# Six raw weight slots in the context pass, and a third of its merge's low parts made by VectorE

## The reference, cut to what matters

```
p = h @ w_in                                   # one projection; its last 4 x 1024 columns are the merge gates
gates = sigmoid(merge_logits.reshape(b, n, 4, 1024))
total = 0.0
for i in range(4):                             # attention, convolution, retention, Fourier
    total = total + gates[:, :, i] * ((ys[i] * silu(zs[i])) @ w_os[i])
y = total @ w_out
```

## Time and profile before

| what | value |
|---|---|
| median of three runs | 2635.76 us |
| lowest and highest | 2635.73 and 2635.92 us |
| span of the profiled execution | 2630.7 us |
| time around the span, median less span | 5.1 us |
| PE busy | 95% of the span |
| POOL busy | 46%, 1114.0 us of it the 818 low parts |
| first gate to last gate of the first pass's merge | from 222.8 to 366.4 us |

### The profile page before, as it was taken

How to read it: one execution, slowest core, us unless ns; L and a number is a source line. 1 busy time by engine, 2 the same in 40 slices (tenths; PEclk the granted TensorE clock), 3 DMA queues, 4 the chain that set the end, 5 groups by cost and what they waited for, 6 DMA issues and landing times.

```text
span 2630.7 us, 39625 instructions
## 1 busy us (share of the span) xinstructions
PE 2498.0 (95%) x12993; PEld 2092.3 (80%) x12993; DVE 1144.0 (43%) x1698; ACT 1114.4 (42%) x2321; POOL 1218.1 (46%) x992
## 2 busy tenths in 40 slices
PE   7888989999999999999999989999999999999997
PEld 1887878799888767787888778898888788888886
DVE  2453565396254433333343365592535423333332
ACT  2645554396221554434433433694214433343332
POOL 1567873222222378855555442122213455555553
PEclk9999999999999999999999989999999999999999
DMA  6345653100121155544433431001211333344333
GB/s 239 93 131 176 197 164 104 40 1 18 48 64 31 57 148 158 158 123 140 137 108 105 140 116 48 13 1 41 62 38 28 108 108 112 111 141 139 109 112 120
DMA packets 391576, 262.37 MB, mean 100 GB/s; under 512 B 16006, under 2 KB 363286, under 8 KB 389914
## 3 DMA queue, kind: packets, MB, share of 16 engines
q1 hardware_dynamic: 377248, 227.07, 29.2%
q10 hardware_dynamic: 14204, 33.67, 3.6%
HBM read 251.23 MB, written 9.45 MB: 99 GB/s over the span
## 4 chain that ended last, share of the span: by engine, by line
PE 79%; issue 7%; POOL 6%; DVE 4%; ACT 2%; DMA 0%; DVEq 0%; POOLq 0%; ACTq 0%; SPq 0%
PE ps L680 76%; POOL w_lo L581 6%; PE ps L839 2%; DVE softmax_stats L1921 1%; DVE r_prev L2028 1%; DVE x_post L2253 0%; DVE a_probT_lo L1662 0%; DMA w_ada<-in_w_ada 0%; PE ps L779 0%; DVE a_out_sum L1662 0%; DVE norm_tmp L1807 0%; PE ps L825 0%; PE ps L712 0%; ACT a_prob L1349 0%; DVE x_post L1766 0%
## 5 line engine op out<-in xcount | busy, mean ns | idle before, releaser
L581 POOL TENSOR_TENSOR w_lo<-w_raw,w_hi 128x512 fp32r<-128x512 f32 x818 | 1114.0, 1373 | 1076.2 <-ACT w_hi L1174 1068.7
L680 PE MATMUL ps<-hT_hi,w_hi 128*128 128x512 f32 (+1 forms) x2528 | 946.1, 374 | 46.9 <-POOL w_lo L581 31.3
L1174 ACT ACTIVATE w_hi<-w_raw 128x512 fp32r<-128x512 f32 x818 | 507.8, 629 | 1010.9 <-PE ps L680 859.1
L680 PE MATMUL ps<-hT_lo,w_hi 128*128 128x512 f32 (+1 forms) x2528 | 932.7, 369 | 0.0
L680 PE MATMUL ps<-hT_hi,w_lo 128*128 128x512 f32 (+1 forms) x2528 | 932.6, 369 | 0.0
L680 PEld LDWEIGHTS ps<-hT_hi,w_hi 128*128 128x128 f32 x2528 | 482.2, 191 | 142.7 <-POOL w_lo L581 31.0
L680 PEld LDWEIGHTS ps<-hT_hi,w_lo 128*128 128x128 f32 x2528 | 482.3, 191 | 79.0
L680 PEld LDWEIGHTS ps<-hT_lo,w_hi 128*128 128x128 f32 x2528 | 482.5, 191 | 75.5
L1662 DVE TENSOR_TENSOR merge_tmp<-merge_tmp,ps 128x512 f32<-128x512 f32 (+1 forms) x160 | 101.5, 634 | 674.5 <-PE ps L680 412.5
L1662 DVE TENSOR_TENSOR merge_tmp<-merge_tmp 128x512 f32<-128x512 f32 (+1 forms) x120 | 168.8, 1406 | 4.1
L680 PE MATMUL ps<-yT_hi,w_hi 128*128 128x512 f32 (+1 forms) x400 | 148.1, 370 | 7.0 <-DVE merge_tmp L1662 3.4
(11 more groups left out here) (265 smaller groups left out, 2799.1 us busy)
## 6 DMA issues: line engine op xcount, KB each, us to landing
w_raw<-in_w_in SPq DMA_DIRECT2D x512, 256.0 KB, 2.9
w_raw<-in_w_o_rest SPq DMA_DIRECT2D x120, 256.0 KB, 2.7
w_raw<-in_w_out SPq DMA_DIRECT2D x80, 256.0 KB, 2.6
w_ada<-in_w_ada SPq DMA_DIRECT2D x8, 1536.0 KB, 9.4
w_raw<-in_w_ada SPq DMA_DIRECT2D x48, 256.0 KB, 2.8
w_raw<-in_w_o_attn SPq DMA_DIRECT2D x40, 256.0 KB, 2.8
w_raw<-in_dft_x SPq DMA_DIRECT2D x16, 256.0 KB, 2.7
gate_row<-gate_rows ACTq DMA_DIRECT2D x5, 512.0 KB, 3.9
```

Source lines behind the costliest of these rows:

```text
L581: eng.tensor_tensor(w_lo[:, r, :], raw[:, r, :], w_hi[:, r, :].bitcast(F32), ALU.subtract).then_inc(sem["w_split"], tally.up("w_split"))
L680: return eng.matmul(dst, lhsT, rhs, start=start, stop=stop)
L1174: return eng.activation(dst, src, func, **kw)
```

## The change

It has two parts. **Six raw slots:** in the first pass the raw ring has HEAD_RING = 6 slots. The two new ones lie in the unused right halves of tiles that the context pass fills only to 256 columns, so each is two pieces of 256 columns, and a unit in such a slot is loaded by two DMAs of half the size; ACT and the low part read it as two pieces in one instruction. SP waits for the unit six before. The first pass's loads and low parts are written out instead of looped. Two token tiles and a gate row are placed elsewhere to make room. **Low parts on VectorE:** in the first pass's merge the low part of each step's third unit, the w_o unit, is made by VectorE (`head_low` in the vector block, 32 of them), and counted on a semaphore of its own, `w_split_dve`. VectorE makes that of step n+1 right after it has added step n's product, ahead of the step's share of `early_norm`, and the first one before the merge's first step. GpSimd leaves these units out. PE and SP wait for the one or the other count.

```diff
+HEAD_RING = 6
...
+        raw_more = [at("w_raw_more0", [P, 2, 512], W + 8704)[:, :, 256:512], at("w_raw_more1", [P, 2, 2048], W + 7680)[:, :, 256:512]]
...
+        total_units, head_units = units, passes[0].units
+        def raw_slot(u):
+            return u % HEAD_RING if u < head_units else u % RING
+        def raw_unit(u):
+            r = raw_slot(u)
+            return raw[:, r, :] if r < RING else raw_more[r - RING]
...
+        def low_by_dve(u):
+            return 0 <= u - first_merge < 12 * KT and (u - first_merge) % 3 == 2
...
@@ sync
+            def free_from(u):
+                if u >= head_units + RING:
+                    eng.wait_ge(sem["w_split"], tally.take("w_split"))
+                    return
+                before = u - (RING if u >= head_units else HEAD_RING)
+                if before >= 0 and low_by_dve(before):
+                    eng.wait_ge(sem["w_split_dve"], dve_lows(before + 1))
+                elif before >= 0:
+                    eng.wait_ge(sem["w_split"], RING + before + 1 - dve_lows(before + 1))
...
-                eng.wait_ge(sem["w_split"], tally.take("w_split"))
+                free_from(u)
...
+                for half in range(2):
+                    if shape == k4:
+                        part, place = src[:, 2 * half:2 * half + 2, :], dst[:, half, :].rearrange("p (k n) -> p k n", n=P)
+                    else:
+                        part, place = src[:, half, :] if shape else src[:, half * 256:(half + 1) * 256], dst[:, half, :]
+                    eng.dma_start(place, part).then_inc(landed[r], tally.up(f"w_landed{r}", 16))
@@ gpsimd
+                while unit[0] < min(last, head_units):
+                    if low_by_dve(unit[0]):
+                        tally.skip("w_high", 1)
+                    else:
+                        head_low(unit[0])
+                    unit[0] += 1
@@ tensor
-                        r = slot()
+                        r = slot(p.opens)
@@ scalar
-                    eng.wait_ge(landed[r], tally.take(f"w_landed{r}", 16))
+                    eng.wait_ge(landed[raw_slot(u)], tally.take(f"w_landed{raw_slot(u)}", 16 if raw_slot(u) < RING else 32))
                     eng.wait_ge(sem["w_used"], tally.take("w_used"))
-                    act(w_hi[:, r, :], raw[:, r, :]).then_inc(sem["w_high"], tally.up("w_high"))
+                    act(split_like(w_hi[:, r, :], u), raw_unit(u)).then_inc(sem["w_high"], tally.up("w_high"))
@@ vector
+            def head_low(u):
+                r = u % RING
+                eng.wait_ge(sem["w_high"], u + 1)
+                tt(split_like(w_lo[:, r, :], u), raw_unit(u), split_like(w_hi[:, r, :], u).bitcast(F32),
+                   ALU.subtract).then_inc(sem["w_split_dve"], tally.up("w_split_dve"))
+
             def merge(p, b):
                 tmp = tmp_blk[b]
                 eng.wait_ge(sem["y_split"], tally.now("y_split"))
+                if p.opens:
+                    head_low(first_merge + 2)
...
                         if more:
                             tally.skip("w_used__done", 2)
+                        if p.opens and 4 * i + j + 1 < 4 * KT:
+                            head_low(first_merge + 3 * (4 * i + j + 1) + 2)
                         if latent:
                             early_norm(i, j)
```

More of the change, by code:

```diff
@@ L220, in trunk @@
         m_gpost = at("mod_gpost", [P, D], W + 6144)
-        m_gate = at("mod_gate", [P, D], W + 7168)
+        m_gate = at("mod_gate", [P, D], W + 12288)
         n_row = at("ada_row", [P, UNIT], Z + 3584)
@@ L334, in trunk @@
         sem = {n: ctx.enter_context(nc.semaphore(n)) for n in names}
-        landed = [ctx.enter_context(nc.semaphore(f"w_landed{r}")) for r in range(RING)]
+        landed = [ctx.enter_context(nc.semaphore(f"w_landed{r}")) for r in range(HEAD_RING)]
         x_in = [ctx.enter_context(nc.semaphore(f"x_in{t}")) for t in range(SEQ // P)]
@@ L380, in trunk, with split_like, dve_lows @@
             units += p.units
-        total_units = units
+        total_units, head_units = units, passes[0].units
[4 more added lines that the diff above has]
+            return raw[:, r, :] if r < RING else raw_more[r - RING]
+        def split_like(t, u):
+            return t if raw_slot(u) < RING else t.rearrange("p (a n) -> p a n", a=2)
+        first_merge = 2 * len(passes[0].tiles) + passes[0].dft
+        def low_by_dve(u):
+            return 0 <= u - first_merge < 12 * KT and (u - first_merge) % 3 == 2
+        def dve_lows(count):
+            return sum(low_by_dve(u) for u in range(count))
         def feeds_next(p, b):
@@ L482, in _ @@
             unit = [0]
+            k4 = {"k": 4, "n": P}
+            def free_from(u):
[7 more added lines that the diff above has]
+                    eng.wait_ge(sem["w_split"], RING + before + 1 - dve_lows(before + 1))
+                if not low_by_dve(u):
+                    tally.take("w_split")
             def load(source, shape=None):
                 src = source() if callable(source) else source
-                r = unit[0] % RING
+                u = unit[0]
+                r, dst = raw_slot(u), raw_unit(u)
                 unit[0] += 1
-                dst = raw[:, r, :]
-                if shape:
+                if r < RING and shape:
                     dst = dst.rearrange(f"p ({' '.join(shape)}) -> p {' '.join(shape)}", **shape)
-                eng.wait_ge(sem["w_split"], tally.take("w_split"))
+                free_from(u)
                 if tally.i is not None:
                     eng.sem_inc(sem["w_slot"], 1)
-                eng.dma_start(dst, src).then_inc(landed[r], tally.up(f"w_landed{r}", 16))
+                if r < RING:
+                    eng.dma_start(dst, src).then_inc(landed[r], tally.up(f"w_landed{r}", 16))
+                    return
+                for half in range(2):
[4 more added lines that the diff above has]
+                    eng.dma_start(place, part).then_inc(landed[r], tally.up(f"w_landed{r}", 16))
             def rounds(times, body, units):
+                if unit[0] < head_units:
+                    for i in range(times):
+                        body(i)
+                    return
                 assert units % RING == 0
@@ L582, in low @@
                                   ALU.subtract).then_inc(sem["w_split"], tally.up("w_split"))
+            def head_low(u):
+                r = u % RING
+                eng.wait_ge(sem["w_high"], tally.take("w_high"))
+                eng.tensor_tensor(split_like(w_lo[:, r, :], u), raw_unit(u), split_like(w_hi[:, r, :], u).bitcast(F32),
+                                  ALU.subtract).then_inc(sem["w_split"], tally.up("w_split"))
             unit = [0]
             def low_parts(last):
+                while unit[0] < min(last, head_units):
[4 more added lines that the diff above has]
+                    unit[0] += 1
                 while unit[0] % RING and unit[0] < last:
@@ L680, in mm, with slot @@
                 return eng.matmul(dst, lhsT, rhs, start=start, stop=stop)
-            def slot():
-                eng.wait_ge(sem["w_split"], tally.take("w_split"))
+            def slot(by_dve=False):
+                if by_dve:
+                    eng.wait_ge(sem["w_split_dve"], tally.take("w_split_dve"))
+                else:
+                    eng.wait_ge(sem["w_split"], tally.take("w_split"))
                 unit[0] += 1
```

12 lines of the change are left out of this document (7 added, 5 removed).

## The result

The changed kernel takes 2622.06 us, the median of four runs (2620.81 to 2626.63), beside 2635.74 us before (four runs, 2632.14 to 2635.92). The ratio is 0.9947 with a 95% interval of 0.9931 to 0.9962: faster, by 13.7 us in the medians. 2622.8 us had been predicted. The first to the last gate of the first pass's merge is 128.6 us, 129.4 had been predicted and 143.6 measured before.

What follows compares the result with a forecast made beforehand. POOL and the raw ring were taken to hold the first pass's merge above PE's pace. Group sums gave 129.4 us against 143.6, 14.2 less, cut to 13.0; span 2630.7 less 13.0, plus 5.1, is 2622.8 us; range 2615 to 2631.

Steps and rivals of the forecast that it cites:

- POOL and the ring are both slower than PE: First pass's merge, per step: POOL 3.9 to 4.1 us and the raw ring 4.10 us, against PE's 3.78 us.
- About 2.5 us of cover: Merge: loads issued two units earlier with six slots are worth about 2.5 us against each late landing.
- So POOL hardly pays: Merge: POOL's low parts run at 1.30 us median beside all DVE work; argued against DVE or port as bound.
- The timing sum: Plain merge steps: DVE's new low part is done at E + 3.2 us, PE needs it at E + 3.6.
- by about 7.4: After a merge group's fourth step: DVE makes the next low part by about E + 7.4 us, PE needs it at 7.9.
- Group 4 starts free: Merge group 4: one low part less and DVE free at its start, so 17.1 us instead of 17.7.
- The low part ahead of the scaling: Merge's end: a DVE low part of 1.0 us in the step before delays what follows by 0.7 to 0.8 us.
- The 5.1 us: Time around the profiled span, said to be left alone by the change and added to 2617.7 us.
- What they did: After the merge: engines of the `w_out` units and next pass do what they did, so the saving moves on whole.
- late landings persist: Rival, chance 0.12: in groups 0, 2 and 3 of the merge losses stay but for about 1 us each; 2628 us.
- VectorE becomes the bound: Rival, chance 0.18: in the merge DVE or the shared port becomes the bound; gain some 5 us, 2630.5 us.
- The strict reading: Merge: each operation holds the shared port for its whole undisturbed length, 15.1 us per group, 17.1 in group 4.

Runs made afterwards that it cites:

- inner: The changed kernel, but the merge's first and last w_o unit get their low parts from GpSimd; ratio to the kernel before 0.9934, merge 126.7 us.
- double: The changed kernel, but VectorE makes each of the 32 low parts twice, first into an unread scratch tile; merge 155.4 us against 128.6.
- again: The changed kernel itself measured once more, nothing altered; median 2623.36 us, ratio to the kernel before 0.9949, merge 128.1 us.
- again_2: The changed kernel measured once more, on the same chip as the mixed kernel with spread tiles; median 2622.05 us, ratio 0.9936, merge 128.1 us.
- mix: Six slots as in the change, but VectorE makes w_o low parts only in groups 1, 3, 5 and 6; ratio to the kernel before 0.9931, merge 125.6 us.
- mix_spread_2: Rerun: six slots, VectorE low parts only in groups 1, 3, 5, 6, first four token tiles loaded one per step; 2614.99 us, ratio 0.9917.
- slots_only: Six raw slots against the kernel before, GpSimd making all low parts; 2622.3 us, ratio 0.9941, merge 128.6 us.
- tiles_spread: The changed kernel, but the four first token tiles are loaded one in each of the first four steps; ratio to the kernel before 0.9922, merge 127.5 us.

## Why the prediction was right

**The total** was right to 0.7 us, and the merge to 0.8 us. The direction and the size of the merge's gain follow from a mechanism that the runs bear out, the ring; that the numbers agree so closely is luck, since errors in several terms cancelled.

**The limits.** The step "POOL and the ring are both slower than PE" was right as a statement of three paces: without the ring, groups 1 and 6 run at 15.8 and 16.8 us, 3.96 and 4.19 us per step, the first inside the 3.9 to 4.1 given for GpSimd, the second a little over. What it left out is that limits in a row don't add: the larger one, the ring with its late landings, hid nearly all of what GpSimd costs. The prediction priced the two parts together and never said what each is worth. One part is worth all of it: six slots alone give the same merge.

**Late landings.** "About 2.5 us of cover" was too small for groups 0 and 2. The sum gave them 2.5 and 3.1 us less by both parts; six slots alone give 3.8 and 3.8, of which the sixth slot has 2.1 and 3.0.

**The low part on VectorE.** 1.0 us was taken, and the mean is 0.96, made of 24 at 0.68 and 8 at 1.76 to 1.78 us; the additions, put at 0.7, fell to a median of 0.43 from 0.90 and a mean of 0.54. "So POOL hardly pays" was wrong: GpSimd's median went from 1.30 to 1.48 us. The timing sum was right for plain groups: the 0.4 us of margin held, PE was busy throughout. (Its "by about 7.4" for the low part after a fourth step is more than its terms make: PE's twelve matmuls end at E + 5.0, product and low part add 1.4, so 6.5; the error was on the safe side.) But the conclusion that nothing is late was drawn for the running merge alone. The first low part, made before the merge's first step, was not looked at: what stands ahead of it in VectorE's queue is the gated tiles' work. That is the missing term, 1.9 us in group 0, shown by inner: it held SP's loads back until the token tiles went out, and it held PE for 3.31 us. It hid in the total, because the cover of the two slots in the same group was 1.3 us too small: 17.8 against the 17.0 predicted. The double run shows how thin the margin is: an operation more on VectorE moves the next one into GpSimd's low part, and costs more than its own length.

**Groups 3 to 5.** 16.5, 17.1 and 18.0 were predicted, 15.9, 18.4 and 16.8 measured; the sum, 51.6, is right to 0.5 us. "Group 4 starts free" was wrong in this profile: VectorE came late out of group 3, and later than in again and again_2.

**The merge's end.** The low part ahead of the scaling was put at 0.7 to 0.8 us. From the last gate to the w_out matmul that follows the seventh set of transposes it is 17.6 us before, 18.1 with six slots alone, in inner and in mix, and 18.6 with the change in all three profiles. So VectorE's last low part costs 0.5 us, and the slots another 0.5, whose cause no run looked for.

**The time around the span.** The 5.1 us were not time outside the span. In each run of the changed kernel the time is 1.8 us over the span, and in those of the kernel before that later batches record it is 2.0 or 2.1; so the profiled execution of before, with its span of 2630.7 us, was a quick one among runs that go from 2632 to 2636 us. The 5.1 were about 3 us too many. The other error is of the same size: the prediction took 13.0 us off the span, and the two profiles differ by 10.2. The two cancelled, which is luck.

**Elsewhere.** "What they did" was right for the work and not for the time. The profiles of before and after differ outside the merge too: its first gate comes 1.7 us later, its tail is 1.0 us longer, and the start of the first latent pass's attention, whose code is the same, is 2.1 us longer. Taken off the merge's 15.1 us, these three leave the 10.2 us by which the spans differ. In the attention the granted clock goes with it, as these windows of the changed kernel show:

```profile
497.73:507.73 10.00, 7.34 (x35) 6.12 (x34) 1.31 (x3) 4.02 (x8) 0.89 (x1) 0.87 0.09 27
507.73:517.73 10.00, 9.51 (x59) 9.07 (x58) 7.00 (x14) 6.89 (x17) 0.88 (x3) 0.78 0.00 0
```

Before, the same work, from 510 to 530 us, stood at 1.00, and in again that start takes 9.0 us, as before (8.9), and not 11.1. So this loss belongs to the execution and not to the change. In again_2 the first gate comes at 229.3 us and in again at 223.7, for one kernel.

**The rivals.** That late landings persist, as one stall of 4.1 us did, and that VectorE becomes the bound, as at the end of group 3, were each partly there. The Trainium skill (SBUF — State Buffer, "Who interferes with whom") says that of a VectorE operation with two inputs in SBUF and a GpSimd one that reads SBUF the one that starts first holds the shared port for its whole length, and the other waits until it is done. That agrees with the lengths of single operations: an addition of 0.42 us takes 1.43 behind a GpSimd low part, and GpSimd's own go to 1.75. The strict reading's 15.1 us of port time per group can't be told from PE's own 15.1: plain groups run at 15.2 to 15.3 us with PE busy throughout. What is refuted is the rival's 16.5 us for them, which added waits between the holders.

## What to carry to other kernels

Before two limits are lifted at once, price each part alone: in a row of waits the longer one hides the other, and here a third slot pair in a ring was worth 15 us of the merge while the second engine's help was worth nothing beside it (4.2 us won in some groups and lost in others) and did harm without it, by its first piece. Given only to the groups in which it helps, in mix, the same help took 3 us off the merge. Work that is moved to another engine is made in that engine's order, so ask what stands ahead of the first and the last piece, not only of the middle ones; and where a slot's release hangs on it, ask what the loader issues next and behind which transfer that falls. A ring needs slots for two things, its steady way round and the longest landing; here a fifth slot was enough for the first, and the second took a sixth.

## What the runs showed of the hardware

A short stall can cost more than itself. After the 1.88 us wait shown above, matmuls with 256 columns went from 0.12 to 0.21 us for about 3 us, and the stretch from 238.4 to 245.8 us has a mean granted clock of 0.77, between the levels of 2.4 and 1.2 GHz. The same kernel in mix_spread_2 had no such stall in group 1, and took 15.0 us for it instead of 18.2. After the 3.31 us wait of the changed kernel matmuls were 0.21 us apart for some 3 us too. It isn't always so: in slots_only and in inner PE waited 1.92 us in group 0, and the granted clock stayed at 1.00.

How much the clock gives differs from run to run in stretches where the work is the same: from 175 to 213 us it is 0.96 before, after and in again, and 0.78 in tiles_spread and in again_2. The first gate comes at 223.7 us in again and at 229.3 in again_2, for one kernel. One profile beside another can so be off by 5.6 us in a stage that nothing has changed, two fifths of this effect; gate-to-gate times of one stage were steadier, 128.6, 128.1 and 128.1 us for the changed kernel.

VectorE's low part of 128x512 took one of two times in the changed kernel: 0.68 or 0.69 us in 24 of 32, 1.76 to 1.78 in the other 8. The addition of 128x256 mostly did too, 0.42 or 1.4 us, but has times between: 0.51 and 1.08 in the changed kernel, and more than half of them before, where GpSimd was in low parts most of the time.
